# The last 16 up chunks of a conv-FFN as Strassen products, on one Trainium2 core

## The reference

```python
def conv_ffn(xn, w_up, conv_w, conv_b, w_down):      # xn [512, 1024], w_up [1024, 2 * 2816]
    h = xn @ w_up
    a, b = jnp.split(h, 2, axis=-1)
    c = lax.conv_general_dilated(a, rhs, ...) + conv_b  # per column, taps t-2, t-1, t
    return (jax.nn.gelu(c, approximate=False) * b) @ w_down

h = h + conv_ffn(rmsnorm(h, ffn_norm_g), ffn_w_up, ffn_conv_w, ffn_conv_b, ffn_w_down)
```

## Time and profile before

| | us |
|---|---|
| median of 3 runs | 1289.22 (1288.03 to 1290.96) |
| the profiled execution's own time | 1291.47 |
| its span, first to last instruction | 1289.7 |
| TensorE busy | 1253.3 (97%) |
| VectorE busy | 699.2 (54%) |
| ScalarE busy | 568.5 (44%) |
| GpSimd busy | 530.7 (41%) |
| mean granted TensorE clock, share of full | 0.997 |
| DMA, mean rate over the span | 128 GB/s |

### The profile page before, as it was taken

One profiled execution on the slowest core, in us unless ns is written; L12 is line 12 of the kernel. 1 busy time (PEld: TensorE's weight loads), 2 busy tenths in 40 slices (PEclk: granted clock), 3 DMA queues, 4 the chain that ended last, 5 costly groups with the idle time before them and its releaser, 6 DMA issues.

```text
span 1289.7 us, 20794 instructions
## 1 busy us (share of the span) xinstructions
PE 1253.3 (97%) x8570; PEld 1019.5 (79%) x8570; DVE 699.2 (54%) x1093; ACT 568.5 (44%) x870; POOL 530.7 (41%) x424
## 2 busy tenths in 40 slices
PE   6999999999999999999998899999999999999999
PEld 5788888866678888767786767788788888888999
DVE  3250004886431266686557657265565665766773
ACT  6541444786665233354544544353422221224452
POOL 6544454322234544534242126331444444546321
PEclk9999999999999999999999999999999999999999
DMA  9836795612115452412220013310222222224554
GB/s 387 348 131 243 248 230 191 163 50 97 51 66 188 122 163 79 181 66 76 69 107 16 3 66 131 135 61 34 99 98 98 81 87 94 99 88 172 166 185 151
DMA packets 24907, 165.05 MB, mean 128 GB/s; under 512 B 2792, under 2 KB 2920, under 8 KB 11504
## 3 DMA queue, kind: packets, MB, share of 16 engines
q1 hardware_dynamic: 20448, 128.15, 27.9%
q10 hardware_dynamic: 2064, 24.07, 5.0%
q0 software_dynamic: 2304, 11.54, 4.5%
HBM read 157.43 MB, written 29.38 MB: 145 GB/s over the span
## 4 chain that ended last, share of the span: by engine, by line
PE 89%; DVE 4%; ACT 3%; POOL 2%; issue 1%; DMA 0%; SPq 0%; DVEq 0%; ACTq 0%
PE banks L488 87%; PE banks L495 2%; DVE arena L1985 1%; POOL h_low L2557 1%; DVE arena L1982 1%; DVE arena L1987 1%; POOL weights_low L2557 1%; DMA arena<-in_mem 0%; ACT weights_high L1192 0%; ACT arena L1238 0%; ACT memory_high L1248 0%; ACT arena L1416 0%; ACT arena L1417 0%; ACT arena L1415 0%; DVE arena L1943 0%
## 5 line engine op out<-in xcount | busy, mean ns | idle before, releaser
L2499 POOL TENSOR_TENSOR weights_low<-weights,weights_high 128x512 fp32r<-128x512 f32 x324 | 433.2, 1367 | 580.5 <-ACT weights_high L1192 580.5
L488 PE MATMUL banks<-h_high_low,weights_high 128*128 128x512 f32 x880 | 358.2, 407 | 1.6 <-ACT arena L1443 1.6
L488 PE MATMUL banks<-h_low,weights_high 128*128 128x512 f32 x880 | 348.9, 397 | 0.0
L488 PE MATMUL banks<-h_high_low,weights_low 128*128 128x512 f32 x880 | 348.8, 396 | 0.0
L1192 ACT ACTIVATE weights_high<-weights 128x2048 fp32r<-128x2048 f32 (+2 forms) x90 | 156.3, 1737 | 243.1 <-PE banks L488 226.0
L488 PEld LDWEIGHTS banks<-h_high_low,weights_high 128*128 128x128 f32 x880 | 166.0, 189 | 46.0 <-issue 5.8
L488 PEld LDWEIGHTS banks<-h_low,weights_high 128*128 128x128 f32 x880 | 166.0, 189 | 41.8 <-issue 3.6
L488 PEld LDWEIGHTS banks<-h_high_low,weights_low 128*128 128x128 f32 x880 | 165.8, 188 | 40.4
L488 PE MATMUL banks<-arena 64*64 64x64 f32 (+6 forms) x1800 | 118.1, 263 | 4.1 <-issue 2.6
L488 PEld LDWEIGHTS banks<-arena 64*64 64x64 f32 (+3 forms) x1800 | 85.9, 148 | 29.9 <-issue 23.2
L1238 ACT ACTIVATE arena<-banks 128x256 f32<-128x256 f32 (+4 forms) x82 | 41.9, 519 | 53.4 <-PE banks L495 35.1
(11 more groups left out here) (360 smaller groups left out, 2371.9 us busy)
## 6 DMA issues: line engine op xcount, KB each, us to landing
weights<-in_stream SPq DMA_DIRECT2D x82, 1024.0 KB, 4.8
sums_kept<-in_down POOLq DMA_DIRECT2D x16, 704.0 KB, 12.8
arena<-in_ada SPq DMA_DIRECT2D x8, 1024.0 KB, 11.9
weights<-in_down SPq DMA_DIRECT2D x9, 704.0 KB, 4.1
weights<-sums_kept SPq DMA_DIRECT2D x9, 704.0 KB, 4.0
sums_kept<-in_down ACTq DMA_DIRECT2D x2, 2816.0 KB, 21.4
sums_kept<-sums_kept ACTq DMA_DIRECT2D x2, 2816.0 KB, 12.6
h<-sums_kept SPq DMA_DIRECT2D x7, 704.0 KB, 4.2
```

The costliest lines, as they stand in the source:

```text
L488: ins = nc.tensor.matmul(o, lhsT, rhs, start=start, stop=stop, skip_group_check=skip)
L2499: nc.gpsimd.tensor_tensor(lo_of(c)[:, cols], raw_of(c)[:, cols], hi_of(c)[:, cols].bitcast(F32), ALU.subtract).then_inc(sem("weights_split ...
```

## The change

The last 16 up chunks (8 of the 11 j) become 16 products c, each with its output tiles, its 512 K halves and the token halves as 2x2 blocks, in 7 pieces of 4 x 3 matmuls of 256 columns. Three j (6 chunks) stay plain. The order of pieces interleaves neighbours: P1, R5 of c, Q4, P3 of c-1, R7, P6, P2 of c. Two pieces share a weight pair of 512 KB; 6 raw and 4 high pair slots lie in the old chunk slots. ScalarE makes a pair's high (`pair_high`), VectorE the low of five pairs in seven, GpSimd of two. ScalarE copies P1 and P1+P6 out of PSUM (`keep`); VectorE makes four outputs and one sum per product (`up_out`, `second_outputs`). Token blocks are normed first (`normed`), and their three sums, highs and lows are made during the plain chunks.

Four sums of up's weights are made in HBM: ScalarE's queue issues two copies of 4 MB behind down's S4 copy, a third after the store of x2, behind a wait for six groups of adds, and a fourth behind the load of `dist`, after a wait for seven. GpSimd issues the adds `add_up`, four DMAs of 1 MB each, and down's S4 add stands two chunks later than before. SyncE waits for all eight groups before the first up piece.

Also: the plain up chunks use six PSUM banks instead of four; ScalarE does the first tap (`tap`) instead of VectorE; `FROM_POOL` of down is every fourth piece only, so the lows of pieces 1 to 3 go to VectorE, ahead of its other work; down's forms are made in another order with the sums in place; some buffers move.

```diff
-STREAM = 85
+UP_PLAIN = 3
+UP = 2 * (KF // 2 - UP_PLAIN)
+STREAM = 63 + 2 * UP_PLAIN
+P1, R5, P3, P6, R7, Q4, P2 = range(FORMS)
+KH, TH = KD // 2, T // 2
+UP_W = KH * P
+UP_STEPS = [[(c, f) for c, fs in ((i, (P1, R5)), (i - 1, (Q4, P3)), (i, (R7, P6, P2))) if 0 <= c < UP for f in fs]
+            for i in range(UP + 1)]
+PAIR_RAW, PAIR_HI = 6, 4
+PAIRS_POOL = [q for q in range(UP_PAIRS) if q % 7 in (2, 5)]
...
-        FROM_POOL = tuple(i for i in range(DOWN) if i < DOWN_PAIRS or i % DOWN_PAIRS == 0)
+        DOWN_FREE = [104, 108, UP_N, UP_N, UP_N]
+        FROM_POOL = tuple(i for i in range(DOWN) if i % DOWN_PAIRS == 0)
...
-            for j in range(KF // 2):
+            M.use([4, 5, 0, 1, 2, 3])
+            for j in range(UP_PLAIN):
...
+            for n, (c, f) in enumerate(UP_SEQ):
+                if f == P6:
+                    pe.wait_ge(sem("up_copied"), 2 * c + 1)
+                elif f == Q4:
+                    pe.wait_ge(sem("product_moved"), moved_at(c, SUM3))
+                elif f == P3:
+                    pe.wait_ge(sem("product_moved"), moved_at(c, C22))
...
+                for k in range(KH):
+                    mm(o, whi[:, k, :], right[0], k == 0 and f not in (P6, Q4, P3), False, skip=True)
+                    mm(o, whi[:, k, :], right[1], False, False, skip=True)
+                    mm(o, wlo[:, k, :], right[0], False, last, sem("product_done") if last else None, skip=True)
...
             act.wait_ge(sem("sums_added"), 3 * 16 * DOWN_PAIRS)
             act.dma_start(sums_kept[S4], sums_kept[S2]).then_inc(sem("sums_copied"), 16)
+            for to in (S1, S3):
+                act.dma_start(up_sums[to], up_in[A21]).then_inc(sem("sums_copied"), 16)
...
             act.dma_start(x2_kept, xres).then_inc(sem("x2_stored"), 16)
+            act.wait_ge(sem("sums_added"), 6 * 16 * DOWN_PAIRS)
+            act.dma_start(up_sums[S2], up_sums[S1]).then_inc(sem("sums_copied"), 16)
             split_weights()
             inverse_rms(3, T, rms2)
...
+            act.wait_ge(sem("sums_added"), 7 * 16 * DOWN_PAIRS)
+            act.dma_start(up_sums[S4], up_sums[S2]).then_inc(sem("sums_copied"), 16)
...
-            low_weights(vb + 3, go)
-            add(S4, A12, 4)
-            low_weights(go, mixers + HI)
+            low_weights(vb + 3, go + 2)
+            add_down(S4, A12, 6)
+            low_weights(go + 2, go + 3)
+            add_up(S1, A22, 6)
+            low_weights(go + 3, go + 4)
+            add_up(S3, A11, 6)
+            low_weights(go + 4, mixers + HI)
...
+            def add_up(to, what, copied):
+                pool.wait_ge(sem("sums_copied"), 16 * copied)
+                for p in range(DOWN_PAIRS):
+                    chunks = slice(UP // 4 * p, UP // 4 * (p + 1))
+                    pool.dma_start(up_sums[to, chunks], up_in[what, chunks], accum_op=ALU.add, max_dma_last_dim=8192)\
+                        .then_inc(sem("sums_added"), 16)
```

More of the change, by code:

```diff
@@ L374, in build @@
+        th_lo = [hl11, ts_lo[0], hl22, ts_lo[1], hl12, ts_lo[2], hl21]
+        th_hi = [hh11, ts_hi[0], hh22, ts_hi[1], hh12, ts_hi[2], hh21]
+        kept1, kept2, kept3 = ([sums[:, i, TH * p:TH * (p + 1)] for p in range(2)] for i in range(3))
+        conv_in = at(SPARE + KH * TH * 6, 3, T + 2)
+        other = nF_rows
         whole = [ctx.enter_context(nc.psum_tensor(f"banks{b}", [P, 2 * T], F32))[:, :] for b in range(0, 8, 2)]
@@ L443, in down_loaded @@
             if s < RAW:
-                return loaded[s], 16 * ((STREAM + i % DOWN_RAW - 2) // RAW + 1 + turn)
+                return loaded[s], 16 * (sum(c % RAW == s for c in range(2, STREAM)) + turn + 1)
             return sem(f"first{s - RAW}_loaded"), 16 * (turn + 2)
@@ new lines, in _ @@
+            split_weights()
+            for m in range(2):
+                tap(m)
+            for m in range(2):
+                gelu(m)
+            split_weights()
+            for i, f in enumerate(T_ORDER):
+                if i == 4:
+                    for m in range(2, 4):
+                        tap(m)
+                act.wait_ge(sem("token_made"), KD + 4)
+                high(th_hi[f], th_raw[f], sem("token_hi"))
+            split_weights()
+            for m in range(2, 4):
+                gelu(m)
@@ new lines, in _, with form_high @@
+            for _ in range(HI):
+                split_weights()
+            assert chunks[0] == STREAM + HI
+            def form_high(f):
+                act.wait_ge(sem("product_done"), UP_N + DOWN_PAIRS * (f - 1))
+                for g, (first, last) in enumerate(GROUPS):
+                    act.wait_ge(sem("forms_made"), {R5: made_at("T1", DOWN_K - 1), P6: made_at("T2", g), R7: made_at("T3", g),
+                                                    Q4: made_at("T4", g)}.get(f, made_at("gact", KF - 1)))
+                    high(t_hi[f % 2][:, first:last, :], form_raw[f][:, first:last, :], sem("forms_hi"))
@@ L1821, in _ @@
+            down_high(1)
+            form_high(R5)
+            for i in range(2, DOWN):
                 down_high(i)
@@ L1823, in _ @@
                 if p == 0 and 2 <= f < FORMS:
[L1824 to L1827 removed]
+                    form_high(f)
         @block.vector
@@ new lines, in low_pair, with to_tile, down_low @@
+            def low_pair(q):
+                if q in PAIRS_DVE:
+                    dve.wait_ge(sem("piece_hi"), q + 1)
+                    low(pair_lo(q), pair_raw(q), pair_hi(q), sem("piece_low"))
+            def to_tile(c, half, side):
+                cols = slice(TH * side, TH * (side + 1))
+                m = up_tile(c, half)
+                return other[:, half, cols] if c % 2 else conv_in[:, m % 3, 2:T + 2][:, cols]
+            def down_low(i):
+                if i < DOWN and i not in FROM_POOL:
+                    dve.wait_ge(sem("piece_hi"), UP_PAIRS + i + 1)
+                    low(down_lo(i), down_raw(i), down_hi(i), sem("piece_low"))
@@ new lines, in gact_out, with normed @@
+            def gact_out(c):
+                for half in range(2):
+                    m = up_tile(c, half)
+                    dve.wait_ge(sem("gelu"), m + 1)
+                    if half == 0:
+                        dve.wait_ge(sem("product_moved"), moved_at(c, C12))
+                    tt(gact_raw[:, m, :], gact_raw[:, m, :], other[:, half, :], ALU.mult).then_inc(sem("forms_made"), 1)
+                    if m >= DOWN_K:
+                        first_form(m)
+            def normed(first, last):
+                for k in range(first, last):
+                    stt(h_raw[:, k, :], xres[:, k, :], par("ffn_g", k), rms[:, :], ALU.mult, ALU.mult)\
+                        .then_inc(sem("token_made"), 1)
@@ new lines, in _ @@
+            dve.wait_ge(sem("token_made"), KD + 2)
+            stt(ts_raw[1], h22, -1.0, ts_raw[0], ALU.mult, ALU.subtract).then_inc(sem("token_made"), 1)
+            dve.wait_ge(sem("token_made"), KD + 3)
+            tt(ts_raw[2], h21, ts_raw[1], ALU.add).then_inc(sem("token_made"), 1)
+            for m in range(2):
+                gact_plain(m)
+            for m in range(2, 4):
+                to_conv(m)
+            for i in range(3):
+                low_tokens(i)
+            for m in range(2, 4):
+                conv(m)
@@ L2697, in lay_stream @@
         parts.append(lay_chunks(np.asarray(a[key])[0], 256))
-    halves = [lay_chunks(up[:, FFN * i:FFN * (i + 1)], 256) for i in range(2)]
+    halves = [lay_chunks(up[:, FFN * i:FFN * i + 256 * UP_PLAIN], 256) for i in range(2)]
     parts.append(np.stack(halves, 1).reshape(2 * halves[0].shape[0], P, -1))
```

470 lines of the change are left out of this document (339 added, 131 removed).

## The result

| | us |
|---|---|
| median after, 4 runs | 1306.72 (1303.78 to 1307.36) |
| median before, 4 runs on the same chip | 1289.87 (1288.03 to 1290.96) |
| ratio | 1.0135, 95% interval 1.0121 to 1.0149 |
| span of the profiled execution, before and after | 1289.7 and 1305.6 |

The change makes the kernel 16.9 us slower; the forecast was 6 us faster, and the range ended at 1294. The page of the kernel after answers to the earlier trace rows: first line busy times, then the DMA queues over the span.

What follows compares the result with a forecast made beforehand. TensorE, busy 97% of the span, was taken to bound the kernel. The terms -21.4 + 1.5 - 2.5 + 3 + 13 = -6.4 us gave 1285.1 from 1291.5, or 1282.9 on the runs' scale; range 1266 to 1294 for 8 in 10.

Steps and rivals of the forecast that it cites:

- part 6: Later sum traffic, third and fourth copies and their adds: each lands over 20 us ahead of its next user; 0.
- part 4: Two 4 MB copies at 391 us: chunk 32's load beside them may land late; +3 us, bounds 0 and 6.6.
- Part 1: Strassen in up: 768 matmuls of 512 columns replaced by 1344 of 256 at 0.1178 us each; -21.4 us.
- Part 2: Feeding up's pieces: small slips of VectorE, +1.5 us, between 0 and 6; token sums in the plain chunks 0.
- part 5: ScalarE's wait after the store of x2: adds land at 548, holding chunk 42's high and the norm; +13 us, bounds 0 and 17.
- Part 3: Start of down: GpSimd makes one of the first four lows, VectorE the others; -2.5 us, gain between 0 and 3.1.
- No hold: Rival at the wait after x2's store: S3's adds land by 534, so no hold; 1269.9 us, chance 0.22.
- VectorE becomes the bound: Rival in up's pieces: VectorE needs 21.3 us a cycle, costing 12 us instead of 1.5; 1293.4 us, chance 0.14.
- Weight loads set the distance: Rival in up's pieces: a 187 ns weight load spaces the matmuls, +72 us instead of -21; 1376 us, chance 0.01.

Runs made afterwards that it cites:

- e6: Kernel after with 8 KB copy packets and the six-group wait moved later, plus the third plain up chunk's high ahead of the token highs: 1273.11 us.
- e5: Kernel after with 8 KB copy packets and the six-group wait moved later, plus lows of down's pieces 1 to 3 back on GpSimd: 1280.28 us.
- e11: Kernel after without the sums of up's weights, only the first two 4 MB copies at 391 us put back in 64 KB packets: 1287.22 us.
- e3: Kernel after, ScalarE's six-group wait and third copy moved behind the first pair of mixers' rates, the dependent add one chunk later: 1295.02 us.
- e7: Kernel after with 8 KB copy packets and the six-group wait moved later, plus all 56 up weight pairs' lows on VectorE: 1275.88 us.
- e12: e10, but of down's lows GpSimd makes only that of piece 0, VectorE the others: 1267.75 us, ratio 0.9839 to the kernel before.
- e10: e6 plus lows of down's pieces 5 and 9 on GpSimd and piece 1's high ahead of the last gelu on ScalarE's queue: 1272.31 us.

## Why the prediction was wrong

Two steps failed above all: part 6's 0 for the later copies, which cost 6.1 us, and part 4's 3 for the first two, which cost 11.5. Both asked too little what small loads wait beside copies in 64 KB packets. Parts 2 and 3 added 1.9 and 5.9.

**Part 1, right.** -20.95 against -21.4; 0.1184 us a matmul over 159.3 us against 0.1178. By the estimate from the Trainium skill, TensorE: Matmul & The Clock Gate, Back-to-back issue gap, a matmul of 256 columns would have cost three quarters of one of 512; it cost half (0.1184 to 0.234) here too.

**Part 2, right in the pieces, short beside them.** No idle of TensorE in the pieces, against 1.5. But I had written off the token sums as 0 because VectorE had room, and looked at VectorE alone. ScalarE's queue was the place: 9.6 us of wait for VectorE's last sum, seven highs, and the chunk's high behind them. It is 3.4 us, 2.2 of them idle, and e6 took it away. The step that failed is the "0": I had asked in part 5 what stands behind a held operation on ScalarE's queue, and did not ask it here.

**Part 3, wrong sign for the stage.** The edit of `FROM_POOL` by itself gained 1.4 to 2.6 us (e5), near the 2.5 of the forecast. What I did not price is the queue that it joins: taps, outputs, two gact tiles, T1's lows and sums all come to VectorE in the same 40 us. I listed VectorE's lows as 1.6 us against a piece's 3.9 and no more. The stage is 3.4 dearer: TensorE's idle is 4.3 instead of 2.5 us, and the granted clock in it 0.98.

**Part 4, the place and the mechanism right, the size wrong by nearly four times.** The sum was 3 with a bound of 6.6; it is 11.5 (11.6 by the table less the 1.4 at S4's copy, 11.5 by e11). I let the landing grow with the bytes of the stream, 17.4 x 1.45 = 25.3; it was 28.1 from 402.55, with the high at 430.73 instead of the 419.9 that was the limit, and a slow clock came on top. The limit of 6.6 was no limit because it rested on one row at 131.64 us. The copies beside that load have smaller packets (2.88 MB in some 64, 45 KB each), and their bytes end at about 145, 13 us behind the load's issue; at chunk 32 they end 24.5 us behind it. And from 0 and 6.6 I took the middle, with no row nearer to 0.

**Part 5, right.** I took 13 from adds landing at 548. They landed at 559.5, with the kernel 12.9 us late by then: 546.6. The hold was 14.91 us and its effect 11.2 at `dist`, 11.7 by e3. By bytes, as chosen.

**Part 6, the step that failed outright.** I gave 0, and argued with the adds' and copies' own deadlines: each lands 20 us ahead of its user. The question to ask was the one of part 4, who else loads at that moment, and what stands behind that load on ScalarE's queue. The fourth copy goes out 0.4 us ahead of a chunk load; the chunk's high holds the queue, and behind it the sums that VectorE and then TensorE need: 6.1 us by the table, some 9 at the place.

**The sum.** -20.95 + 3.4 + 3.4 + 11.5 + 11.2 + 6.1 + 1.4 (already at S4's copy, spread between executions) = +16.1, against +15.9 in the spans. The forecast had -6.4. Of the 22.5 between them 8.5 come from part 4, 6.1 from part 6, 5.9 from part 3, 1.9 from part 2 (3.4 beside the pieces, less the 1.5 for them), 1.4 are the spread ahead of the first copy, 0.5 come from part 1, and part 5 was 1.8 too high.

**The rivals.** "No hold" fell with the 205 GB/s of the adds. By the rate of the Trainium skill, DMA: Bandwidth & Descriptors, Measured, 425 GB/s, it would have come true; that figure is for plain loads, and the trace of after speaks against it for adding DMAs as that of before did. "VectorE becomes the bound" fell with e7. "Weight loads set the distance" fell with part 1. What happened, three front costs together, was in none of them: every rival stood in the new stage or at the one wait I had seen, none in the loads of others. The range left out the end that part 4's and part 6's terms would have had with honest bounds.

## What to carry to other kernels

A bulk copy has two prices: its own landing, and what each small load beside it waits; the second goes by the size of its packets (13 us at 8 KB and 28 at 64 KB for a 1 MB load that takes 5 alone, beside 8 MB of copies), so issue background copies in packets of the size of the loads that matter, and check each one, late ones too, against the loads asked for in its time. A wait in a queue is priced by all that stands behind it, for whichever engine; put it behind the last thing that someone needs. And lows given to GpSimd to spare VectorE can cost VectorE as much as they save: with 8 KB packets, the three repairs of order and GpSimd out of down but for piece 0, e12 is 1.6% faster than the kernel before (0.9839), 20.8 us, about what the pieces save.

## What the runs showed of the hardware

**Packet size against other queues' loads**, above: 4.8 us alone, 13.3, 20.6 and 28.1 beside 8, 32 and 64 KB packets, at equal bytes; one packet for one (115 to 115, 65 to 65, 111 to 112), and no packet of the load in the first 4 us.

**The clock after an idle.** TensorE had been idle 9.45 us at 434.08. The granted clock (the column behind TensorE's busy time) is 0.50, its level of 1.2 GHz, in the first 3 us after it, and 1.00, 2.4 GHz, from 440 on:

```profile
434.10:437.00 2.90, 2.90 (x7) 0.50 0.30 51
437.00:440.00 3.00, 3.00 (x11) 0.79 0.71 300
440.00:445.00 5.00, 5.00 (x23) 1.00 0.01 3
```

At 1.00 there is a matmul each 0.234 us, 4.0 us for 17; here the 17 from 434.08 to 440.02 took 5.9, 2.0 more. So the idle of 9.45 us costs 11.4. The restart at 563.61 looks the same (0.50 for 3.4 us, 0.84 for the next 3).

**VectorE beside GpSimd**: the earlier trace rows had one collision, 1.51 us where the like takes 0.41. Over a whole stage it is 15 us of VectorE for 48 us of GpSimd (e7), and 1.3 to 1.9 times the duration where GpSimd doesn't pause (e10, e12). All these have both inputs in SBUF; the outputs with an input in PSUM, among the same rows of e10, keep their 0.41 us. By the Trainium skill, GPSIMD Engine Reference, Specifications, VectorE contends with GpSimd in instructions with two SBUF inputs or in a two-port mode. The rows agree for two SBUF inputs; they show nothing of the modes.
